# Moving tiles of the up, down and in2 projections, and the high gate weights, placed 16 to 64 bytes later in SBUF

## What is computed

```
h @ w_in[l]                                   # first block: mixer inputs and 48 gate tiles of 128 columns
up = causal_dwconv(h @ w_up, conv_w, conv_b)  # 2048 -> 2 * 5632, "up"
(jax.nn.silu(a) * b) @ w_down                 # 5632 -> 2048, "down"
```

## Time and profile before

| | |
|---|---|
| median of 3 runs | 2975.9 us (2974.11 to 2978.74) |
| profiled execution, first to last instruction (span) | 2978.0 us |
| PE busy | 2946.2 us, 99% of the span |
| PEld (weight loads) | 2630.0 us |
| DVE, ACT, POOL busy | 2051.0, 1311.7, 70.0 us |
| mean granted TensorE clock | 0.998 |

### The profile page before, as it was taken

How to read it: one execution, slowest core, us unless ns; L and a number is a source line. 1 busy time by engine, 2 the same in 40 slices (tenths; PEclk the granted TensorE clock), 3 DMA queues, 4 the chain that set the end, 5 groups by cost and what they waited for, 6 DMA issues and landing times.

```text
span 2978.0 us, 47097 instructions
## 1 busy us (share of the span) xinstructions
PE 2946.2 (99%) x18616; PEld 2630.0 (88%) x18616; DVE 2051.0 (69%) x2624; ACT 1311.7 (44%) x1418; POOL 70.0 (2%) x72
## 2 busy tenths in 40 slices
PE   8999999999999999999999999999999999999999
PEld 8898898999988888888888888876998888888888
DVE  6675787977788888885557776636666666666444
ACT  5354423444444444444444354425445444444333
POOL 0000000000001000000000000000000000000000
PEclk9999999999999999999999999999999999999999
DMA  6553334555555555555555544531555555555555
GB/s 230 184 183 134 114 120 149 168 173 198 186 196 193 189 196 194 190 182 190 193 195 198 195 172 168 186 122 43 184 198 186 195 197 188 193 197 177 194 193 184
DMA packets 87359, 530.39 MB, mean 178 GB/s; under 512 B 9952, under 2 KB 10336, under 8 KB 41184
## 3 DMA queue, kind: packets, MB, share of 16 engines
q1 hardware_dynamic: 87264, 529.07, 50.7%
HBM read 526.94 MB, written 2.10 MB: 178 GB/s over the span
## 4 chain that ended last, share of the span: by engine, by line
PE 96%; DVE 2%; ACT 1%; DMA 0%; issue 0%; SPq 0%; DVEq 0%; ACTq 0%
PE bank L576 74%; PE late L576 22%; DVE arena L1687 1%; DVE w_low L1687 0%; DVE half_low L1687 0%; DVE arena L1684 0%; ACT w_high L1203 0%; PE late L1144 0%; DVE arena L1989 0%; DMA ring<-in_w_gates 0%; DMA xT<-in_xT 0%; DVE acts_both L1687 0%; DVE arena L2045 0%; DVE arena L2016 0%; DVE xrs L1734 0%
## 5 line engine op out<-in xcount | busy, mean ns | idle before, releaser
L1687 DVE TENSOR_TENSOR w_low<-ring,w_high 128x2048 fp32r<-128x2048 f32 (+1 forms) x480 | 1014.3, 2113 | 384.1 <-ACT w_high L1203 380.2
L1203 ACT ACTIVATE w_high<-ring 128x2048 fp32r<-128x2048 f32 (+1 forms) x480 | 849.5, 1771 | 636.0 <-DMA ring<-in_w_down 223.0
L576 PE MATMUL bank<-up_early,w_high 128*128 128x512 f32 x1408 | 487.8, 389 | 0.0
L576 PE MATMUL bank<-up_late,w_high 128*128 128x512 f32 x1408 | 487.3, 389 | 0.0
L576 PE MATMUL late<-acts_both,w_high 128*128 128x512 f32 x1408 | 479.0, 389 | 0.3 <-DVE w_low L1687 0.3
L576 PE MATMUL bank<-up_early,w_low 128*128 128x256 f32 x1408 | 388.6, 276 | 0.0
L576 PE MATMUL late<-acts_both,w_low 128*128 128x256 f32 x1408 | 388.6, 276 | 0.0
L576 PE MATMUL bank<-up_late,w_low 128*128 128x256 f32 x1408 | 388.6, 276 | 0.0
L576 PEld LDWEIGHTS bank<-up_early,w_high 128*128 128x128 f32 x1408 | 264.5, 188 | 55.2
L576 PEld LDWEIGHTS late<-acts_both,w_high 128*128 128x128 f32 x1408 | 264.3, 188 | 55.1 <-DVE w_low L1687 0.6
L576 PEld LDWEIGHTS bank<-up_late,w_high 128*128 128x128 f32 x1408 | 264.0, 188 | 54.7
(11 more groups left out here) (311 smaller groups left out, 4946.2 us busy)
## 6 DMA issues: line engine op xcount, KB each, us to landing
ring<-in_w_up SPq DMA_DIRECT2D x176, 1024.0 KB, 4.7
ring<-in_w_down SPq DMA_DIRECT2D x128, 704.0 KB, 4.0
ring<-in_w_in SPq DMA_DIRECT2D x66, 1024.0 KB, 4.7
ring<-in_w_mix SPq DMA_DIRECT2D x62, 1024.0 KB, 4.8
ring<-in_w_gates SPq DMA_DIRECT2D x96, 512.0 KB, 3.7
ring<-in_w_branch SPq DMA_DIRECT2D x16, 1024.0 KB, 4.7
ring<-in_w_out SPq DMA_DIRECT2D x16, 1024.0 KB, 4.8
ring<-in_w_o SPq DMA_DIRECT2D x16, 1024.0 KB, 4.8
```

The costliest lines, as they stand in the source:

```text
L576: return nc.tensor.matmul(o, lhsT, rhs, start=first, stop=last)
L1203: A(w_high[:, s, 0:cols], ring[:, s, 0:cols], ACT.Copy).then_inc(rounded[s], 1)
L1687: return V.tensor_tensor(o, a, b, op)
```

## The change

Five placements move, nothing else. The moving pairs of up begin 80 bytes past a multiple of 128 (a view that starts 4 elements into a tensor placed 64 bytes on), `in2_early` 32 bytes, `in2_mid`, the activations of down (their float32 view `ACTS` too) and `half_high` 64 bytes. `in2_next`, `in2_late`, the mixer's, branches' and out's tiles, `w_low`, `half_low` and `w_high` keep their place relative to multiples of 128. Behind the ring and behind hT a pad of 128 bytes makes room for what now reaches past their ends, so hT begins 128 bytes and the arena 256 bytes later than before. The arena is 256 bytes (64 of its 33744 columns) shorter.

On every engine the instructions, their order, their shapes and their waits are the same as before; only addresses differ. So there are no moved rows to show.

```diff
+IN2_SHIFT, UP_SHIFT, ACTS_SHIFT = 32, 80, 64
...
         ring = sb("ring", [P, RING, UNIT])
         ring_base = nc.sbuf_base - RING * UNIT * 4
+        sb("ring_pad", [P, 32])
         xT = sb("xT", [P, KT, T])
         hT = sb("hT", [P, KT, T])
         hT_base = nc.sbuf_base - KT * T * 4
+        sb("hT_pad", [P, 32])
...
-        in2_early = alias("in2_early", hT_base, [P, 8, 2, T])
-        in2_mid = alias("in2_mid", arena_base, [P, 3, 2, T], 88)
+        in2_early = alias("in2_early", hT_base, [P, 8, 2, T], 0, IN2_SHIFT)
+        in2_mid = alias("in2_mid", arena_base, [P, 3, 2, T], 88, ACTS_SHIFT)
...
-        half_high = alias("half_high", ring_base, [P, RING, HALF], 2 * UNIT // T)
+        half_high = alias("half_high", ring_base, [P, RING, HALF], 2 * UNIT // T, 64)
...
-        up_early, up_late = alias("up_early", hT_base, [P, 8, 2, T]), alias("up_late", arena_base, [P, 8, 2, T], 78)
+        up_early, up_late = (alias(name, base, [P, 16 * T + 8], at, UP_SHIFT - 16)[:, 4:4 + 16 * T]
+                             .rearrange("p (k a t) -> p k a t", a=2, t=T)
+                             for name, base, at in (("up_early", hT_base, 0), ("up_late", arena_base, 78)))
...
-        acts_both = alias("acts_both", arena_base, [P, 2, FF_TILES, T], 0)
+        acts_both = alias("acts_both", arena_base, [P, 2, FF_TILES, T], 0, ACTS_SHIFT)
...
-        ACTS = tiles(0, FF_TILES)
+        ACTS = tiles(ACTS_SHIFT // 4, FF_TILES)
```

## The result

The changed kernel takes 3019.3 us (median of 4 runs, 3016.4 to 3022.1) against 2977.3 us for the kernel before (4 runs, 2974.1 to 2985.7). The ratio is 1.0143, with a 95% interval of 1.0123 to 1.0162. The prediction was 2948 us, faster. The kernel became 42 us slower, outside the range of the prediction and on the other side of no change.

A forecast was written before the change was run, and what follows sets the result against it. TensorE's distances between matmul starts were taken to bound the kernel; savings of 6 (gates), 18.8 (up) and 3.1 us (in2_early) summed to 27.9, taking the 2978.0 span to 2950.1 and the median to 2948 us, range 2904 to 2984.

The forecast's parts named there:

- Distance 0 costs 13.3, distance 64 costs 6.7 to 10.4: Extra ns per weight load, by the distance between the starts of the moving and the loaded tile modulo 128.
- moving them apart by any part of the period should do: Premise for up's pairs: any distance but 0 costs what 64 costs, saving 6.7 ns a pair.
- Modulo 128: In all matmul stages, the extra cost was taken to depend on the moving-to-loaded tile distance modulo 128 bytes.
- Pads: 0: Pads behind the ring and hT: distances modulo 128 stay in the unshifted stages, so no cost, 0 us.
- Up, -18.8: Up's 2816 pairs, shifted 80 bytes, were each to save 6.7 ns, 18.8 us in all.
- in2_early, -3.1, in2_mid, 0: in2: 464 early pairs save 6.7 ns each, 3.1 us; 174 mid pairs only swap distances 0 and 64, 0 us.
- Down, 0: Down's 1408 pairs swap distances 0 and 64, so the sum of the two prices stays: 0 us.
- the bound of 12 us: Down's possible loss if its long matmul took 235 ns at distance 64: 1408 x 8.4 ns.
- Gates, -6: 1536 loads of half_high go from distance 0 to 64 and save 4.5 to 10.1 us, taken as 6.
- Slower: Rival, chance 0.13: tiles starting inside a 64-byte stretch make both loads cost as distance 0; up and in2_early lose, 2992 us.
- Deep gain: Rival, chance 0.20: only starts at multiples of 64 collide; up and in2_early save 14.6 ns a pair, 2922 us.
- The two notes: Skill pages quoted against the forecast: independent read ports, so time stays 2976 us; a gap formula giving 325 ns a pair.

The follow-up runs named there:

- experiment 9: Kernel before plus, behind its last down, single matmul streams at 16 distances and 24 pairs at each of 64 places, twice; the added stretch took 1258 us.
- experiment 1: Changed kernel with its two pads alone, every shift zero; 3003.8 us, ratio 1.0072 against the kernel before.
- experiment 5: Changed kernel with hT and the arena both moved by 256 bytes and only half_high shifted; 2979.7 us against 2982.9 for the kernel before, ratio 0.9992.
- experiment 7: Changed kernel without shifts, pad of 128 bytes behind the ring and none behind hT, every pair at (128, 64); one run, 3027.7 us.
- experiment 6: Changed kernel with all its shifts but pads of 256 bytes each; 3029.4 us, ratio 1.0160 against the kernel before.
- experiment 15: Changed kernel with pads of 256 bytes each and only up shifted, by 80 bytes; 3019.4 us, ratio 1.0146 against the kernel before.
- experiment 13: Kernel before plus, behind its last down, 16 pairs at each of 256 places, twice; 512 readings from 340.0 to 360 ns a pair, no kernel time given.
- probe: Matmul streams added behind the last down of the kernel before to read prices by placement; one added stretch took 1258 us, no whole-kernel time given.
- experiment 3: Changed kernel with the pads alone, and everything from the ring on 64 bytes later; 3000.5 us, ratio 1.0064 against the kernel before.
- experiment 10: Kernel before with a small extra matmul ahead of most weight units of both downs; 2987.9 us against 2973.8.

## Why the prediction was wrong

What bounds the kernel, the reading of pairs at 340 ns, and that other engines do not matter all held. The clock was not the full one throughout, as I read it: it was granted at half for 3.4 us at 318, 3.4 at 383 and 6.8 at 2021, a few us in all. What failed is the price list and with it every term that rested on it.

- **"Distance 0 costs 13.3, distance 64 costs 6.7 to 10.4."** This is the step that failed. I read the 13.3 from matmuls of 256 columns and gave it to the load of `w_low`, which falls under the matmul of 512. There distance 0 costs 226.7 - 213.3 = 13.4 ns too, but is the least of the list, whose other values go up to 21.3 (experiment 9). The 6.7 that I then took as what is left is right in size for the short matmul (113.3 - 106.7 = 6.6), and is the least of that list. What I took as one dear and one cheap load was the minimum of both lists, so that "moving them apart by any part of the period should do", the premise of the 6.7 ns saved for each pair of up, could only turn out the other way: up's pairs became 8.3 to 13.3 ns dearer. The warning was in the earlier trace rows: 21.7 ns extra under 512 columns at distances 0 and 64 alike. I kept it as a bound and not as what it was, the ordinary price under a long matmul.
- **"Modulo 128."** The period is 256 bytes (experiments 1, 5, 7). Before, I had only tiles at multiples of 128 with one exception, so no row could tell 128 from 256.
- **"Pads: 0."** Wrong: hT moved by 128 against the ring. Alone this costs 27.7 us by steps, 6.8 of them the first down at its slower speed, and by time 20.7 us, ratio 1.0072. The sign that I had named for it, that mix and out would move, could not show it: their tiles lie in the arena, which the pads moved by 256, and both stayed. In the changed kernel it can't be added to the shifts: the pads and the shifts together cost 42 us, the shifts alone 47 (experiment 6).
- **Up, -18.8.** Measured +25.9. At clean pads it is +37.5 (experiment 15).
- **in2_early, -3.1, in2_mid, 0.** Measured about +7 for all of in2.
- **Down, 0.** Measured +14.2; the bound of 12 us that I gave it for a price of 235 ns was nearly this, and 233.5 ns is what its long matmul took in the second block.
- **Gates, -6.** Measured -4.4: the one term with the right sign and size. It rested on the earlier trace rows, the same width on both sides. With the pads alone the gates already give some 2.3 us of this (experiment 1); with the shift alone they give 4.4 (experiment 5), so the two, 6.7 in sum, do not add. `half_low`, which was not to move, went from 120.0 to 118.6; the pads alone take it to 119.3 and the shift alone to 119.5, and the two together would make 118.8. Its weight loads fell with the others, from 194 ns to 190, where I had expected that of `half_high` alone.
- **The rivals.** "Slower" had the sign, 2992 us and a chance of 0.13. Its mechanism (a tile off a multiple of 64 touches one stretch more) is not what happened: tiles at (128, 64) and (0, 128), all on multiples of 64, lose as much or more (one run each, 3027.7 and 3037.2 us). "Deep gain" hoped for the floor of 325; over 512 readings nothing came under 340.
- **The two notes.** The Trainium skill, "SBUF — State Buffer", "Who interferes with whom", has TensorE's two read ports independent and TensorE waiting for nobody. The traces disagree with the first: with all other engines idle, the pairs of experiment 13 took 340 to 360 ns by placement alone. The Trainium skill, "TensorE: Matmul & The Clock Gate", "Back-to-back issue gap", would give 325 ns a pair by its formula, which it calls the gap of an isolated matmul; no stream of pairs in any run here is so quick (the least is 340.0).

**What stays open.** Why distance 0 is dear under 256 columns and cheap under 512; why a pair's price is not a sum; why probe and kernel differ at some places; and what picks the speed at a start. The runs show that it is picked there and held. That the groups of run times, 2996.4 and 2996.9 against 3004.0 and 3004.4 in experiment 3, are a down at one speed or the other (703 pairs by 9.7 ns is 6.8 us) is argued: I have a profile at 340 for the quicker group and none of the slower one. The clock, granted at 0.999 in all four, is not what parts them. In the changed kernel it may be: the two runs at 3016.4 and 3016.5 had 0.999 and 1.000, the two at 3022.0 and 3022.1 had 0.998.

## What to carry to other kernels

A price read from one instruction's shape is not that of another's: before a placement is costed, measure a stream of the very pair at a grid of placements, behind the end of the kernel, where one run reads all of them. Take what it gives as a list of candidates and run the best in the kernel itself: (0, 192) had 340.0 in the probe and 350.0 in the kernel. Where a kernel's speed per pair is a round number that stays the same in every stage (340.0 here), ask whether it already stands at a minimum, since a shift then has only one way to go. A pad that makes room is a change of placement too: keep the tiles' distances modulo 256, or whatever period the runs show, and cost the pad alone.

## What the runs showed of the hardware that I had not expected

- **Two speeds at one placement.** Pairs at (0, 64) run at 340.0 or 350.0 ns, chosen when the stream starts after a wait and held (11 and 5 of 16 streams). A matmul put into a stream at 340 does not change it.
- **A period of 256 bytes** between the moving and the loaded tile: moving hT by 128 costs 11.4 ns for each pair of up_early, moving it and the arena by 256 nothing.
- **Many means lie on a grid.** 113.3, 116.7, 120.0, 226.7, 233.4, 340.0, 346.7, 350.0 and 353.3 ns are, within 0.1, multiples of 3.33 ns, eight periods of the granted 2.4 GHz; 340.0 and 346.7 are 102 and 104 of them. Two thirds of the 512 readings of experiment 13 are such multiples; others, as 348.9 and 351.1, are not.
- **What suits one width hurts the other.** 256 columns: 113.3 at distance 64, 120.0 at 0. 512 columns: 226.7 at 0, 233.4 at 32.
- **A short matmul between pairs costs more than its own length.** 16 columns take 27 ns and the two pairs behind it another 99 (experiment 10).
